# DeltaNet gate stores of the odd units moved from the ScalarE queue to SyncE, between the weight loads and the small matrix stores

## The chip, the core and the metric

One core of one Trainium2 chip runs the kernel. The metric is the device time in microseconds (us) of one execution; the time before is the median of three runs. One further execution was profiled.

## What is computed

The reference is a trunk of two layers. Each layer has two token mixers side by side, retention and a gated DeltaNet, on a sequence of 1024 tokens with 1024 channels, in float32. Cut to the part that the change touches:

```python
proj = rmsnorm(x, norm_g) @ w_in
(rq, rk, rv, rz, dq, dk, dv, dz, db, da, gr, gd) = jnp.split(proj, _split_points(), axis=-1)
# retention -> o_r;  DeltaNet over 8 heads in chunks -> o_d, with for each chunk
#   L = strict lower part of (k_beta k^T) * decay;  solve (L + I) [u w] = rhs
y = jax.nn.sigmoid(gr) * (o_r @ w_up_r) + jax.nn.sigmoid(gd) * (o_d @ w_up_d)
return x + y @ w_o
```

The two merge gates `gd` and `gr` are columns of the one input projection. They come early and are needed late, at the merge.

## The kernel before

**Tiling.** Activations lie transposed, channels on the 128 partitions and tokens along the row, in two halves of 512 tokens. Each float32 operand is split into a high and a low part, so that a dense block of 128 output channels takes, for each half, 8 channel tiles with three matmuls each (lines 846, 848 and 850): 24 matmuls into one of two PSUM banks, `dense_ps[0]` for half 0 and `dense_ps[1]` for half 1. One weight buffer, `w_raw`, takes a 512 KB weight block. ScalarE copies it to `w_hi` (line 1409) and GpSimd makes `w_lo` (line 2543); then `w_raw` is free for the next load.

**Units.** The DeltaNet has 8 heads of two halves, so 16 units in each layer. `unit_schedule` writes out the order of the work for all engines: while the scan of one unit runs (steps `ks`, `xu`, `so` for each of its four chunks), the solve of the next unit is prepared, and pieces of dense blocks fill TensorE in between. Even units (of the schedule) carry the dense blocks K, Z, Q of the next head; odd units carry V, D, R, where D is the DeltaNet merge gate `gd` and R the retention merge gate `gr`.

**The gates.** ScalarE takes a tanh of each half of D and R out of PSUM into the buffer `gate_t[:, half, :]` (line 1521) and then frees the PSUM bank. The buffer is shared by D, R and Z, so each tanh first waits (`gt_st[half]`) until the store of what lay there has landed. The stores go to the scratch tensor `gate_dram` in DRAM, 256 KB each. In the odd units the two D stores are issued by ScalarE itself right behind the tanh (line 1526), the two R stores by SyncE (line 744).

**The small matrices.** Of each chunk the solve needs the 16x16 diagonal blocks of L. VectorE computes them (line 2159, signal `nl_ok`), SyncE writes them to DRAM with eight 4 KB DMAs (`l_store`, line 705), waits until they have landed, and loads them again, broadcast over the partitions, with two 256 KB DMAs (`l_load`, line 713). VectorE then runs 15 steps of forward substitution (lines 2244 and 2247), among which it does its part of the scan: line 2263 makes `uu`, for which the matmul of step `xu` waits (line 1162), and line 2278 updates the state.

**SyncE's queue** works strictly in program order, waits included. For head h it is, in `unit_loads`: weight load Q, row load, weight loads V and D, blocks of unit 2h+2, weight load R, row load, the weight loads m+6 and m+7 (K and Z of the next head; Z or a retention block for the last), blocks of unit 2h+3, and the two R stores. "Odd matrix" below is the set of blocks of unit 2h+3. There are 7 such heads in each layer, so 14 in all. A weight load waits until `w_lo` of the block before it is ready (line 635).

Of the kernel before, what the change touches and what calls it, by code (L numbers as in the profile page):

```python
# [23 lines left out]
HALF = 512  # L24
NHALF = SEQ // HALF
# [3 lines left out]
DH = 8  # L29
# [252 lines left out]
def build(nc, x, norm_gain, w_in, conv_w, a_log, dt_bias, dn_gain, w_up_ret, w_up_dn, w_out, final_gain,  # L282
          masks, rope, ret, out):
    ctx = ExitStack()
    with ctx:
# [3 lines left out]
        def signal(name, per):  # L289
            s = Signal(ctx.enter_context(nc.semaphore(name)), per)  # L290
            signals.append(s)
            return s
# [39 lines left out]
        def ar(name, shape, dt=F32):  # L332
            n = int(np.prod(shape[1:]))
            a = place["at"]
            place["at"] = a + n
            assert place["at"] <= ARENA, (name, place)
            if dt is F32:
                v = arena[:, a:a + n]
                if len(shape) == 3:
                    v = v.rearrange("p (a b) -> p a b", a=shape[1])  # L340
                if len(shape) == 4:
                    v = v.rearrange("p (a b c) -> p a b c", a=shape[1], b=shape[2])
                return v
            return nc.alloc_sbuf_tensor_at(name, shape, dt, offset=arena_at + 4 * a)
# [8 lines left out]
        gate_t = ar("gate_t", [P, 2, HALF])  # L353
# [134 lines left out]
        gate_dram = nc.dram_tensor("gate_scratch", [2, KT, P, SEQ], F32)  # L488
# [43 lines left out]
        gt_ok = signal("gate_tanh_ready", 4)  # L532
        gt_st = [signal("gate_stored0", 32), signal("gate_stored1", 32)]
# [82 lines left out]
        def w_src(t, what, col=0):  # L616

            return what[t, :, bass.ds(col, P)].rearrange("(k p) n -> p k n", p=P)
# [3 lines left out]
        def _(eng):  # L622
# [9 lines left out]
            def load_w(g, src, other=False, ahead=0):  # L632

                eng.wait_ge(w_lo_ok.sem, w_lo_ok.after(g, -ahead))
                eng.dma_start(w_from[other][:, :, :], src).then_inc((w2_in if other else w_in_ok).sem, 16)
# [41 lines left out]
            for l in range(DEPTH):  # L677
# [12 lines left out]
                def row_load(h, b):  # L690

                    u = (l * (2 * DH) + (2 * h + b))
                    eng.wait_ge(m_ok.sem, m_ok.after(u, 0))
                    eng.wait_ge(egc_ok.sem, egc_ok.after(u, 0))
                    eng.dma_start(gcb, row_dram[bass.ds(h, 1), b * HALF:(b + 1) * HALF].to_broadcast([P, HALF]))\
                       .then_inc(row_in.sem, 16)

                def l_store(u, half):

                    t = (l * (2 * DH) + u)  # L700
                    eng.wait_ge(nl_ok.sem, nl_ok.after(t, 1))
                    eng.wait_ge(l_in.sem, l_in.after(t, 0))
                    for a in range(NB if u else NB // 2):
                        seg = slice(BASE * a, BASE * (a + 1))
                        eng.dma_start(l_dram[a].rearrange("c i k -> i c k"), nl[half][seg, :, seg]).then_inc(l_st.sem, 16)

                def l_load(u):

                    t = (l * (2 * DH) + u)
                    eng.wait_ge(l_st.sem, l_st.after(t, 16 * NB))  # L710
                    eng.wait_ge(sv_s.sem, sv_s.after(t, 0))
                    for c in range(0, CPH, 2):
                        eng.dma_start(lb[:, c:c + 2, :], l_source(c)).then_inc(l_in.sem, 16)

                def l_blocks(u, half):
                    l_store(u, half)
                    l_load(u)
# [7 lines left out]
                def unit_loads(h, more):  # L725
                    m = (n + h * 6)
                    load_w(m + BLK_HEADS + 2, w_src(l, w_in, DQ0 + P + h * P))
                    row_load(h + 1, 0)
                    load_w(m + BLK_HEADS + 3, w_src(l, w_in, DV0 + P + h * P))
                    load_w(m + BLK_HEADS + 4, w_src(l, w_in, GD0 + P + h * P))  # L730
                    l_blocks(2 * h + 2, 0)
                    load_w(m + BLK_HEADS + 5, w_src(l, w_in, GR0 + P + h * P))
                    row_load(h + 1, 1)
                    if more:
                        load_w(m + BLK_HEADS + 6, w_src(l, w_in, DK0 + 2 * P + h * P))
                        load_w(m + BLK_HEADS + 7, w_src(l, w_in, DZ0 + P + h * P))
                    else:
                        load_w(m + BLK_HEADS + 6, w_src(l, w_in, DZ0 + P + h * P))
                        load_w(m + BLK_HEADS + 7, w_src(l, w_in, RK0))
                    l_blocks(2 * h + 3, 1)  # L740
                    hc = l * DH + h + 1
                    for b in range(NHALF):
                        eng.wait_ge(gt_ok.sem, gt_ok.after(hc, 3 + b))
                        eng.dma_start(gate_dram[1, bass.ds(h + 1, 1), :, b * HALF:(b + 1) * HALF]
                                      .rearrange("k p t -> p (k t)"), gate_t[:, b, :]).then_inc(gt_st[b].sem, 16)

                for h in range(DH - 2):
                    unit_loads(h, True)
# [588 lines left out]
        def _(eng):  # L1337
# [53 lines left out]
            for l in range(DEPTH):  # L1391
                n = l * NBLK

                def raw_evac(g, t, i):

                    j, b = i // 2, i % 2
                    eng.wait_ge(dense_ok[b].sem, dense_ok[b].after(g, 1))
                    eng.wait_ge(conv_s.sem, conv_s.after(t, 8 if j == 2 else 0))
                    eng.activation(raw[:, j % 2, 3 + b * HALF:3 + (b + 1) * HALF], dense_ps[:, b, :], ACT.Copy)\  # L1399
                       .then_inc(raw_ok.sem, 1)  # L1400
                    eng.wait_ge(raw_ok.sem, raw_ok.after(t, i + 1))
                    eng.sem_inc(dense_free[b].sem, 1)
# [67 lines left out]
                def delta_unit(kind, h):  # L1470

                    b = 0 if kind in ("even", "even_last") else 1
# [5 lines left out]
                    t = (l * (2 * DH) + (2 * h + b)) if kind != "first" else None  # L1478
                    hn = (l * DH + (h + b))
                    hz = (l * DH + h) if kind != "first" else None  # L1480
                    hc = (l * DH + (h + 1))
                    for step in unit_schedule(kind):
# [17 lines left out]
                        elif what == "evac":  # L1500
                            blk, of, half = step[1:]
                            gg = g + (g0 + blk)
                            if of in "KQV":
                                raw_evac(gg, hc, 2 * "KQV".index(of) + half)
                            elif of == "Z":

                                eng.wait_ge(dense_ok[half].sem, dense_ok[half].after(gg, 1))
                                eng.wait_ge(sz_ok.sem, sz_ok.after(hn, 0))
                                eng.wait_ge(gt_st[half].sem, gt_st[half].after(hc, 0))
                                eng.activation(gate_t[:, half, :], dense_ps[:, half, :], ACT.Tanh, scale=0.5)\  # L1510
                                   .then_inc(zt_ok.sem, 1)
                            elif of in "DR":

                                a = "DR".index(of)
                                if kind == "first" and a and half:
                                    eng.wait_ge(w_lo_ok.sem, w_lo_ok.after(n + BLK_HEADS + 1, 0))
                                    eng.dma_start(w_raw[:, :, :], w_src(l, w_in, DZ0)).then_inc(w_in_ok.sem, 16)
                                eng.wait_ge(dense_ok[half].sem, dense_ok[half].after(gg, 1))
                                eng.wait_ge(sz_ok.sem, sz_ok.after(hc, 0))
                                eng.wait_ge(gt_st[half].sem, gt_st[half].after(hc, 16 * a))  # L1520
                                eng.activation(gate_t[:, half, :], dense_ps[:, half, :], ACT.Tanh, scale=0.5)\
                                   .then_inc(gt_ok.sem, 1)
                                eng.wait_ge(gt_ok.sem, gt_ok.after(hc, 2 * a + half + 1))
                                eng.sem_inc(dense_free[half].sem, 1)
                                if kind == "first" or a == 0:
                                    eng.dma_start(gate_dram[a, bass.ds(h + 1, 1), :, half * HALF:(half + 1) * HALF]
                                                  .rearrange("k p t -> p (k t)"), gate_t[:, half, :])\
                                       .then_inc(gt_st[half].sem, 16)
                            elif of in ("rk", "rq"):
                                ret_swap(l * RH, gg, ("rk", "rq").index(of), half)  # L1530
                            else:
                                ret_v(l * RH, gg, int(of[2]), half)
# [179 lines left out]
                for i in range(NHALF * KT):  # L1712
                    b, j = i // KT, i % KT
# [1026 lines left out]
```

## Time and profile before

| | |
|---|---|
| median of 3 runs | 2662.98 us (2661.4 to 2663.35) |
| profiled execution, its own time | 2656.2 us |
| its span, first to last instruction | 2654.4 us |
| TensorE (PE) busy | 2636.3 us, 99% |
| VectorE (DVE) busy | 1728.7 us, 65% |
| GpSimd (POOL) busy | 818.7 us, 31% |
| ScalarE (ACT) busy | 686.0 us, 26% |
| granted TensorE clock | 0.999 |
| DMA queue q1 (SyncE) | 159.07 MB |
| DMA queue q10 (ScalarE) | 56.15 MB |

How to read it: a share is the time in which an engine had work, over the whole span. In a list of waits a row says who waited, for whom, how long in total, how often, and the longest. In a timeline a row has the start, the time from the first to the last of its instructions, the engine, the line and operation with output and inputs, the count, and in brackets idle time of the engine just before, with what ended it. SPq and ACTq are DMA issues in the queues of SyncE and ScalarE, PEld is TensorE's weight load. Matmuls are pipelined: each row of PE overlaps the next, and starts lie some 0.23 us apart in a dense block.

### The profile page before, as it was taken

How to read it: one execution, taken by the hardware profiler on the slowest of the kernel's cores; microseconds unless marked ns; L12 is line 12 of the kernel's file. 1: busy time of each engine (PE TensorE's matmuls, PEld its weight loads, DVE VectorE, ACT ScalarE, POOL GpSimd, SP SyncE). 2: the span in 40 equal slices, each digit the busy share in tenths (PEclk: the TensorE clock that was granted, in tenths of full speed). 3: DMA queues.
4: the chain of work that ended last, by engine and by line, in shares of the span. 5: the costliest groups of instructions: out<-in, count | busy, mean ns of one | idle time of the engine just before them, and what ended most of it. 6: DMA issues, size and time to landing. Idle time of an engine off the chain costs nothing.

```text
span 2654.4 us, 40007 instructions
## 1 busy us (share of the span) xinstructions
PE 2636.3 (99%) x14874; PEld 2256.0 (85%) x14874; DVE 1728.7 (65%) x3866; ACT 686.0 (26%) x1376; POOL 818.7 (31%) x451
## 2 busy tenths in 40 slices
PE   8999999999999999999999999999999999999998
PEld 6888888888898899888878888888888998898887
DVE  7878777877756655434578778777877555563333
ACT  5323233333212222200143333333232221231001
POOL 3123333333312212434512332332323122232453
PEclk9999999999999999999999999999999999999999
DMA  5321223122211112433533222222222111133344
GB/s 174 98 85 55 83 65 89 53 85 65 84 40 53 32 42 71 129 97 117 163 91 95 68 76 66 72 77 69 69 69 78 45 50 43 40 106 99 98 137 151
DMA packets 293413, 217.77 MB, mean 82 GB/s; under 512 B 31746, under 2 KB 246100, under 8 KB 292964
## 3 DMA queue, kind: packets, MB, share of 16 engines
q1 hardware_dynamic: 259620, 159.07, 20.7%
q10 hardware_dynamic: 33600, 56.15, 6.2%
q8 instruction: 119, 1.95, 0.3%
q14 instruction: 74, 0.61, 0.1%
HBM read 176.30 MB, written 38.86 MB: 81 GB/s over the span
## 4 chain that ended last, share of the span: by engine, by line
PE 96%; DVE 1%; DMA 1%; ACT 1%; issue 0%; SPq 0%; POOL 0%; DVEq 0%; ACTq 0%
PE dense_ps L846 24%; PE dense_ps L850 23%; PE dense_ps L848 23%; PE work L829 3%; PE dense_ps L870 2%; PE dense_ps L871 2%; PE dense_ps L872 2%; PE work L1125 1%; PE work L1084 1%; PE work L1162 1%; PE work L1182 1%; PE work L1101 1%; PE work L1151 1%; PE work L1175 1%; PE work L1121 1%; PE work L1136 1%
## 5 line engine op out<-in xcount | busy, mean ns | idle before, releaser
L846 PE MATMUL dense_ps<-act_hi,w_hi 128*128 128x512 f32 x2552 | 1049.3, 411 | 0.8 <-POOL act_lo L2564 0.7
L850 PE MATMUL dense_ps<-act_hi,w_lo 128*128 128x512 f32 x2552 | 999.3, 392 | 0.0
L848 PE MATMUL dense_ps<-act_lo,w_hi 128*128 128x512 f32 x2552 | 997.5, 391 | 0.0
L2543 POOL TENSOR_TENSOR w_lo<-w_raw,w_hi 128x1024 fp32r<-128x1024 f32 x162 | 399.6, 2467 | 1004.8 <-ACT w_hi L1409 562.3
L850 PEld LDWEIGHTS dense_ps<-act_hi,w_lo 128*128 128x128 f32 x2552 | 479.4, 188 | 106.5
L846 PEld LDWEIGHTS dense_ps<-act_hi,w_hi 128*128 128x128 f32 x2552 | 481.3, 189 | 84.6 <-POOL act_lo L2564 2.3
L848 PEld LDWEIGHTS dense_ps<-act_lo,w_hi 128*128 128x128 f32 x2552 | 481.9, 189 | 79.3 <-issue 0.5
L1943 DVE SCALAR_TENSOR_TENSOR arena<-arena,cols 128x512 f32<-128x512 f32 x288 | 240.5, 835 | 5.2
L1409 ACT ACTIVATE w_hi<-w_raw 128x1024 fp32r<-128x1024 f32 x94 | 99.1, 1054 | 329.9 <-PE dense_ps L850 310.8
L1399 ACT ACTIVATE arena<-dense_ps 128x512 f32<-128x512 f32 x96 | 57.2, 596 | 270.1 <-PE dense_ps L850 270.1
L829 PE MATMUL work<-mk,arena 128*128 128x128 f32 x768 | 112.2, 275 | 7.9 <-DMA arena<-in_x 7.9
L1957 DVE SCALAR_TENSOR_TENSOR arena<-arena 128x512 f32<-128x512 f32 x96 | 112.0, 1166 | 11.2 <-ACT arena L1415 10.9
L2244 DVE TENSOR_TENSOR arena<-arena 128x60 f32<-128x60 f32 (+14 forms) x480 | 99.6, 208 | 20.8 <-DMA arena<-l_scratch 8.4
L2630 POOL TENSOR_TENSOR arena<-arena,negh 128x4 f32<-128x4 f32 x32 | 38.7, 1211 | 240.8 <-DVE arena L2150 240.8
L872 PE MATMUL dense_ps<-v_later_lo,act_hi 128*128 128x256 f32 x384 | 107.9, 281 | 0.0
L870 PE MATMUL dense_ps<-v_later_hi,act_hi 128*128 128x256 f32 x384 | 107.9, 281 | 0.0
L871 PE MATMUL dense_ps<-v_later_hi,act_lo 128*128 128x256 f32 x384 | 107.9, 281 | 0.0
L829 PEld LDWEIGHTS work<-mk,arena 128*128 128x128 f32 x768 | 91.9, 142 | 17.7 <-issue 5.1
L2247 DVE TENSOR_TENSOR arena<-arena 128x60 f32<-128x60 f32 (+14 forms) x480 | 92.5, 193 | 16.5
L846 PE MATMUL dense_ps<-o_hi,w_hi 128*128 128x512 f32 x256 | 99.6, 389 | 0.0
L848 PE MATMUL dense_ps<-o_lo,w_hi 128*128 128x512 f32 x256 | 99.6, 389 | 0.0
L850 PE MATMUL dense_ps<-o_hi,w_lo 128*128 128x512 f32 x256 | 99.6, 389 | 0.0
(257 smaller groups left out, 4014.8 us busy)
## 6 DMA issues: line engine op xcount, KB each, us to landing
w_raw<-in_w_in SPq DMA_DIRECT2D x138, 512.0 KB, 3.8
arena<-l_scratch SPq DMA_DIRECT2D x64, 256.0 KB
arena<-gate_scratch ACTq DMA_DIRECT2D x64, 256.0 KB, 2.8
gate_scratch<-arena ACTq DMA_DIRECT2D x36, 256.0 KB, 2.0
w_raw<-in_w_out SPq DMA_DIRECT2D x18, 512.0 KB, 3.7
o_scratch<-arena ACTq DMA_DIRECT2D x32, 256.0 KB, 2.0
w_raw<-in_w_up_dn SPq DMA_DIRECT2D x16, 512.0 KB, 3.7
arena<-o_scratch ACTq DMA_DIRECT2D x32, 256.0 KB, 3.6
```

The source lines that it names most:

```text
L829: mm = eng.transpose(wk[bank][:, c * P:(c + 1) * P], src, ident)
L846: eng.matmul(dense_ps[:, to, :], w_hi[:, slot, k, :], hi[:, k, seg], start=(k == 0), stop=False)
L848: eng.matmul(dense_ps[:, to, :], w_hi[:, slot, k, :], lo[:, k, seg], start=False, stop=False)
L850: mm = eng.matmul(dense_ps[:, to, :], w_lo[:, slot, k, :], hi[:, k, seg], start=False, stop=(k == KT - 1))
L870: eng.matmul(dst, act_hi[:, k, tok], hi[:, k, :], start=(k == 0), stop=False)
L871: eng.matmul(dst, act_lo[:, k, tok], hi[:, k, :], start=False, stop=False)
L872: mm = eng.matmul(dst, act_hi[:, k, tok], lo[:, k, :], start=False, stop=(k == KT - 1))
L1409: eng.activation(w_hi[:, slot, :, :], w_raw[:, :, :], ACT.Copy).then_inc(w_hi_ok.sem, 1)
L1943: eng.scalar_tensor_tensor(out=acc[:, i % 2, :], in0=src, scalar=wcol, in1=acc[:, i % 2, :], op0=ALU.mult, op1=ALU.add).then_inc(conv_s.se ...
L1957: eng.scalar_tensor_tensor(out=kqv[:, i // 2, i % 2 * HALF:(i % 2 + 1) * HALF], in0=th[:, i % 2, :], scalar=1.0, in1=acc[:, i % 2, :], op0 ...
L2244: eng.tensor_tensor(xm[:, :, 0:left], column, xs[:, :, k:k + 1].to_broadcast([P, CPH, left]), ALU.mult).then_inc(sv_s.sem, 1)
L2543: eng.tensor_tensor(w_lo[:, slot, :, :], w_from[second][:, :, :], w_hi[:, slot, :, :].bitcast(F32), ALU.subtract)\
```

## The change

The two D stores of every odd unit are no longer issued by ScalarE. SyncE issues all four gate stores: the two of D behind the weight load m+7 and ahead of the blocks of the odd matrix, the two of R behind these as before. The first unit of a layer keeps its four stores on ScalarE. Sizes, destinations and counts stay.

```diff
@@ SyncE, unit_loads
+                    hc = l * DH + h + 1
+
+                    def gate_store(a, b):
+                        eng.wait_ge(gt_ok.sem, gt_ok.after(hc, 2 * a + b + 1))
+                        eng.dma_start(gate_dram[a, bass.ds(h + 1, 1), :, b * HALF:(b + 1) * HALF]
+                                      .rearrange("k p t -> p (k t)"), gate_t[:, b, :]).then_inc(gt_st[b].sem, 16)
+
+                    gate_store(0, 0)
+                    gate_store(0, 1)
                     l_blocks(2 * h + 3, 1)
-                    hc = l * DH + h + 1
-                    for b in range(NHALF):
-                        eng.wait_ge(gt_ok.sem, gt_ok.after(hc, 3 + b))
-                        eng.dma_start(gate_dram[1, bass.ds(h + 1, 1), :, b * HALF:(b + 1) * HALF]
-                                      .rearrange("k p t -> p (k t)"), gate_t[:, b, :]).then_inc(gt_st[b].sem, 16)
+                    gate_store(1, 0)
+                    gate_store(1, 1)
@@ ScalarE, delta_unit, D and R
-                                if kind == "first" or a == 0:
+                                if kind == "first":
                                     eng.dma_start(gate_dram[a, bass.ds(h + 1, 1), :, half * HALF:(half + 1) * HALF]
```

## Rows read from the trace of the kernel before

**Rows 1.** The page: the span, and TensorE's busy time, share and instructions.

```profile
span 2654.4 us, 40007 instructions
PE 2636.3 (99%) x14874; PEld 2256.0 (85%) x14874; DVE 1728.7 (65%) x3866; ACT 686.0 (26%) x1376; POOL 818.7 (31%) x451
```

**Rows 2.** Timeline of SyncE's queue around the end of one odd unit.

```profile
339.99 19.22 SPq L635 DMA_DIRECT2D w_raw<-in_w_in  x2
359.31 3.80 SPq L705 DMA_DIRECT2D l_scratch<-arena  x8
364.15 1.21 SPq L713 DMA_DIRECT2D arena<-l_scratch  x2
365.41 0.93 SPq L744 DMA_DIRECT2D gate_scratch<-arena  x2
```

**Rows 3.** Timeline of ScalarE, same unit: second D store, tanh of R's halves.

```profile
353.71 0.33 ACTq L1526 DMA_DIRECT2D gate_scratch<-arena  x1
...
359.48 0.60 ACT L1521 ACTIVATE arena<-dense_ps 128x512 f32<-128x512 f32 x1 [2.45 <-PE dense_ps L850]
364.93 0.60 ACT L1521 ACTIVATE arena<-dense_ps 128x512 f32<-128x512 f32 x1 [4.84 <-PE dense_ps L850]
```

**Rows 4.** Timeline of GpSimd and VectorE, same unit: `w_lo`, blocks, first solve step, `uu`.

```profile
356.41 2.39 POOL L2543 TENSOR_TENSOR w_lo<-w_raw,w_hi 128x1024 fp32r<-128x1024 f32 x1
...
356.61 1.11 DVE L2159 SCALAR_TENSOR_TENSOR arena<-work,arena 128x128 f32<-128x128 f32 x4
...
371.12 0.26 DVE L2244 TENSOR_TENSOR arena<-arena 128x60 f32<-128x60 f32 x1 [0.28 <-DMA arena<-l_scratch]
...
376.53 0.34 DVE L2263 SCALAR_TENSOR_TENSOR arena<-work,arena 128x128 f32<-128x128 f32 x1
```

**Rows 5.** Timeline of TensorE, same unit: first matmul of K, and step `xu`.

```profile
364.73 0.39 PE L846 MATMUL dense_ps<-act_hi,w_hi 128*128 128x512 f32 x1
...
377.04 0.39 PE L850 MATMUL dense_ps<-act_hi,w_lo 128*128 128x512 f32 x1
377.27 0.38 PE L1162 MATMUL work<-arena 128*128 128x128 f32 x2
```

**Rows 6.** Issue to landing, minimum, median, maximum: R stores, ScalarE's gate stores, load m+7.

```profile
DMA to landing us min/median/max: 5.1/6.0/6.4
...
DMA to landing us min/median/max: 2.0/2.0/5.4
...
DMA to landing us min/median/max: 3.7/3.7/3.7
```

**Rows 7.** Two stretches of 1 us, same unit; the last columns are clock, DMA share, GB/s.

```profile
361.00:362.00 1.00, 1.00 (x6) 0.81 (x5) 0.00 (x0) 0.00 (x0) 0.00 (x0) 1.00 1.11 305
...
364.00:365.00 1.00, 1.00 (x6) 0.81 (x6) 0.00 (x0) 0.07 (x1) 0.00 (x0) 1.00 0.00 0
```

**Rows 8.** VectorE's waits in the stretches of the 14 odd matrices, one layer each.

```profile
DVE arena L2244 <- DMA arena<-l_scratch: 1.3, 3, 0.6
DVE arena L2244 <- DMA arena<-l_scratch: 1.4, 3, 0.8
```

**Rows 9.** Timeline, odd unit with the longest such wait: solve start, `uu`, step `xu`.

```profile
1593.24 0.26 DVE L2244 TENSOR_TENSOR arena<-arena 128x60 f32<-128x60 f32 x1 [0.81 <-DMA arena<-l_scratch]
...
1598.66 0.34 DVE L2263 SCALAR_TENSOR_TENSOR arena<-work,arena 128x128 f32<-128x128 f32 x1
...
1598.63 0.39 PE L850 MATMUL dense_ps<-act_hi,w_lo 128*128 128x512 f32 x1
1599.06 0.49 PE L1162 MATMUL work<-arena 128*128 128x128 f32 x2
```

**Rows 10.** Timeline, last odd matrix of layer 2: solve start, step `xu`.

```profile
2040.56 0.26 DVE L2244 TENSOR_TENSOR arena<-arena 128x60 f32<-128x60 f32 x1 [0.42 <-DMA arena<-l_scratch]
...
2047.31 0.49 PE L1162 MATMUL work<-arena 128*128 128x128 f32 x2 [0.40 <-DVE arena L2263]
```

**Rows 11.** Timeline of VectorE, an odd matrix without such a wait: solve start.

```profile
281.26 0.24 DVE L2244 TENSOR_TENSOR arena<-arena 128x60 f32<-128x60 f32 x1
```

## The prediction

> **What bounds the kernel now.** I read the page first. TensorE is busy for 2636.3 of 2654.4 us [rows 1], and the granted clock is full. Nothing that only frees another engine can shorten this; a change moves the time if it makes TensorE wait, or removes one of its few waits. So I read next, unit by unit, how close the other engines come to making it wait, on SyncE's queue, then ScalarE, VectorE and TensorE in the same stretch. The odd unit at 340 to 378 us stands for the 14. SyncE issues the weight load m+7 as the second of the two in the first row, at 359.21 - 0.38 = 358.83 us, once `w_lo` is done (356.41 + 2.39 = 358.80) [rows 2, 4]. The eight block stores follow at once, although their data were ready at 357.72 [rows 2, 4]. They take 3.80 us to issue, 1.04 us pass until they have landed, and the block loads are issued at 364.15 to 365.36. The solve starts at 371.12, and VectorE had waited 0.28 us for just these loads [rows 4]. This is the reading that matters: **the chain load m+7, block stores, block loads, solve has no slack of its own on VectorE** in this unit. Over the 14 odd matrices such a wait stands in six, 1.3 + 1.4 = 2.7 us together [rows 8].
>
> How much of it TensorE sees: among the solve steps VectorE makes `uu`, at 376.53 to 376.87, and the matmul of `xu` starts at 377.27, one pitch of 0.23 us behind the matmul ahead of it, so with no wait [rows 4, 5]. In the unit with the longest wait, 0.81 us, `uu` ends at 1599.00 and `xu` starts at 1599.06, where 1598.63 + 0.23 = 1598.86 was due: 0.20 late [rows 9]. So a gap up to 0.61 us is free there, and beyond it each part is paid by TensorE; the matmul then also shows 0.49 instead of 0.38 us [rows 5, 9], which I count as 0.11 more. The last matrix of a layer has other VectorE work in front, and there 0.42 us of gap goes with 0.40 us of TensorE idle [rows 10]: no part is free.
>
> **The change part by part.** Per odd unit it removes two DMA issues from ScalarE (0.33 us each, [rows 3]) and adds two to SyncE.
>
> *ScalarE's part.* 28 x 0.33 = 9.2 us of issue go from an engine that is busy 26% of the time [rows 1] and has idle time of 2.45 and 4.84 us ahead of the next two tanh [rows 3]. Since TensorE waits for none of that, I take nothing. The bound is a gain of 9.2 us if all of it stood on the path; no row shows any of it there.
>
> *SyncE's part.* The D halves have long been converted when SyncE gets past load m+7 (the second store was issued at 353.71 before [rows 3]), so the two added waits cost nothing. The two issues do: two R stores from SyncE take 0.93 us [rows 2], and with the semaphore waits between I take 1.0 us. The bounds are 2 x 0.33 = 0.65 us (ScalarE's price, [rows 3]) and 1.1 us. I stay with SyncE's own row, as the same instruction on the same queue. Queued behind them are the block stores, which were ready 1.1 us before they were issued, so that they move by the full 1.0 us; behind them the wait for their landing, the block loads, and the R stores. The next weight load is issued 3 us after the R stores and isn't moved. The DMA engines show a share of 0.00 from 364 to 365 [rows 7], so the block stores aren't held back by anything that a later issue would dodge: they land 1.0 us later, the loads too.
>
> *The stores' place.* They queue behind the 512 KB of load m+7, which lands 3.7 us after its issue, at 362.5 [rows 6]. 256 KB at the 305 GB/s of the best stretch [rows 7] are 0.86 us, so the D stores land near 363.4 and 364.3. The first is awaited by R's first tanh, at 359.48 now, which must be done before the first matmul of block K at 364.73 [rows 3, 5]: it may start at about 364.0. So the tanh slips by 4 us and hides in the 4.84 us of idle, with 0.6 us to spare. The second tanh is due at 364.93, with 0.6 us to spare also. For the landing the bounds are 2.0 us (a gate store alone) and 6.4 us (an R store behind the block loads) after issue [rows 6]. My value lies between, since only the weight load is ahead. Before, the same stores ran when the engines were empty. On this the Trainium skill, page DMA: Bandwidth & Descriptors, section Issuing engines are not separate DMA queues, says that DMAs of all issuing engines share the same 16 engines, so that another issuer saves only the issue time of its sequencer. The 2.0 against 6.0 us agree if the difference is what lay ahead [rows 6]. By that rule the change hands issue time to the sequencer that has none to spare, which is the same sum.
>
> **The sum.** With every gap 1.0 us longer, a regular unit pays gap + 1.0 - 0.61 + 0.11 = gap + 0.5.
> - Five regular units with a visible gap: 2.7 less 0.42 for the last matrix is 2.3 us; 2.3 + 5 x 0.5 = 4.8, less the 0.3 that the 0.81 us unit pays already: 4.5 us.
> - Seven regular units without a wait in the list. There the loads landed some unknown time before the solve. One began its solve at 281.26 [rows 11], so its landing lies before that. The visible ones are nearest, so I take 0.1 us ahead, 0.4 us each: 2.8 us. Bounds 0 and 0.5 each.
> - The last matrices, where nothing is free: 1.0 and, without a visible gap, 0.9 (bounds 0.5 and 1.0): 1.9 us.
>
> Together 9.2 us. The profiled execution's own 2656.2 us would be 2665.4; it lies 6.8 us under the median of the runs, and I add the sum to the median: 2662.98 + 9.2 = 2672.2 us. TensorE's stalls do not give back anything later, since every later step of TensorE is in order and already dense.
>
> **The rivals.**
> - *A, the forecast*: the block stores leave later and TensorE waits at `xu`. With an issue price of 0.9 to 1.1 us and landings that scatter by 0.3 us, 2668.5 to 2679.
> - *B, not slower by what can be measured*: the delay is smaller than the slack. If the issue costs ScalarE's price, the delay is 0.65 us, and the sum is 2.3 + 5 x 0.15 - 0.3 = 2.8, plus 7 x 0.15 = 1.0, plus 0.65 and 0.5: 5 us, so 2668. If in addition the block loads land faster, because load and R stores meet less of the next weight load, up to all of it is hidden: 2663. For it speaks that eight of the 14 show no wait. Against it, that the row of SyncE says 0.93, and that six are at the edge. It decides below a delay of 0.65 us.
> - *C, the stores' landing*: if the D stores land like the R stores, 6.4 us after 359.31, R's first tanh starts at 365.7 in place of the permitted 364.0: 1.7 us in each of 14 units, 24 us, so 2687. The block path would then hide behind it. Or the block stores' completion waits for the D stores: with the second D store landing at 366.2 the loads are issued 1.05 us later than I say, 14 x 1.05 + 9.2 = 24 us, again 2687. It decides once the D stores land later than 4.7 us after their issue. The same page of the Trainium skill, section Queues, rings and completion order, says that a DMA's semaphore write lands only after every earlier write of that DMA engine. By that rule the big stores ahead could hold the small ones' signals; no row of before has a big write ahead of the block stores.
> - *D, faster*: ScalarE's 9.2 us are worth something. Bound 2654, no row speaks for it.
>
> **How the numbers follow.** A 0.69, B 0.21, C 0.07, D 0.03. The predicted time is that of A. Everything under 5.3 us (0.2%) either way is about what a measurement of this kernel cannot tell from no change. A and C give slower, B gives same: slower 0.75 (with the part of B that lies at its upper end and less the low end of A), same 0.22, faster 0.03. The range goes from 2664, which takes in the larger part of B, to 2682, which takes in A with all its upper bounds and leaves C out.
>
> **What would show it.** Right: in each of the 14 units SyncE's first block store starts some 1.4 to 1.5 us after load m+7's issue instead of 0.48; the list of waits has VectorE line 2244 waiting for the block loads in all 14, 12 to 17 us together instead of 2.7; TensorE or its weight load waits at line 1162 for line 2263 in nearly all of them; the tanh of R's first half starts some 4.5 us after load m+7's issue, with no idle time of TensorE at the first matmul of K. Wrong: a block store less than 0.7 us later (B), the D stores landing over 4.7 us after issue or the wait for the block stores much over 1.04 us (C), or a gap at line 2244 that grew by 1 us while TensorE shows no wait at line 1162, which would mean that I took VectorE's slack too small.

## The result

The changed kernel takes 2676.88 us (median of 4, 2675.96 to 2678.66) beside 2662.19 us before (median of 4): the ratio is 1.0065, with a 95% interval of 1.0053 to 1.0077, so 14 to 20 us slower. The two profiled executions, 2656.2 and 2675.96 us, lie 19.8 us apart. The forecast was slower by 9.2 us, to 2672.2 us in a range of 2664 to 2682: the direction and the range hold, and the size was taken more than a third too small (9.2 us beside 14.7 us by the medians and 17.3 us by the ratio).

The page after, answering to [rows 1]:

```profile
span 2674.2 us, 40007 instructions
PE 2642.4 (99%) x14874; PEld 2252.2 (84%) x14874; DVE 1729.5 (65%) x3866; ACT 686.2 (26%) x1376; POOL 818.3 (31%) x451
```

The share of busy time hides the loss: 99% both times. TensorE's busy time grew by 6.1 us with the same instructions. Of this, 6.0 us stand at steps `ks` and `xu`: a matmul that comes late is itself longer (0.38 for 0.27 us at `xu`), and it no longer overlaps the one ahead of it. TensorE's list of waits has the rest of the loss. Before, this list had only one wait of 0.4 us for line 2263 among the solve steps. Lines from 744 on are shifted by 6, so 1157 is the old 1151 (step `ks`), 1168 the old 1162 (step `xu`), 2250 the first operation of the solve (2244), 2269 makes `uu` (2263) and 2284 updates the state (2278). TensorE's waits after, over the span, without those of the start:

```profile
PE work L1157 <- DVE arena L2284: 7.0, 13, 1.1
PE work L1168 <- DVE arena L2269: 5.7, 14, 0.4
```

Both wait for VectorE operations that stand among the solve steps, which start late. VectorE's waits for the block loads in the stretches of the 14 odd matrices, answering to [rows 8]:

```profile
DVE arena L2250 <- DMA arena<-l_scratch: 14.1, 7, 2.6
...
DVE arena L2250 <- DMA arena<-l_scratch: 12.5, 7, 2.3
```

26.6 us in all 14 units, in place of 2.7 us in six. Where they come from stands in SyncE's queue, same unit as [rows 2], and the next line is VectorE's first solve step, as in [rows 4]:

```profile
342.88 19.21 SPq L635 DMA_DIRECT2D w_raw<-in_w_in  x2
362.14 1.05 SPq L744 DMA_DIRECT2D gate_scratch<-arena  x2
363.29 4.12 SPq L705 DMA_DIRECT2D l_scratch<-arena  x8
368.60 1.21 SPq L713 DMA_DIRECT2D arena<-l_scratch  x2
369.86 0.94 SPq L744 DMA_DIRECT2D gate_scratch<-arena  x2
...
375.39 0.26 DVE L2250 TENSOR_TENSOR arena<-arena 128x60 f32<-128x60 f32 x1 [1.66 <-DMA arena<-l_scratch]
```

Load m+7 is issued at 342.88 + 19.21 - 0.38 = 361.71. Counted from there, and beside [rows 2]: the block stores start at 1.58 us (0.48 before), they take 4.12 us (3.80 before), and from their end to the block loads 1.19 us pass (1.04 before). So the block loads leave 6.89 us after load m+7, 5.32 before: 1.57 us later, and only 1.10 of that is the two D stores and the waits between them. The rest is new: **the same eight stores are slower to issue and slower to land behind the D stores' data.** Two stretches of 1 us show why (columns as in [rows 7]):

```profile
365.00:366.00 1.00, 1.00 (x6) 0.83 (x5) 0.00 (x0) 0.00 (x0) 0.00 (x0) 1.00 1.12 404
366.00:367.00 1.00, 1.00 (x6) 0.82 (x5) 0.00 (x0) 0.37 (x1) 0.00 (x0) 1.00 0.83 235
```

These are 3.3 to 5.3 us after load m+7. The same time in the kernel before, 362 to 364 us, was nearly free of data:

```profile
362.00:364.00 2.00, 2.00 (x10) 1.68 (x9) 0.00 (x0) 0.00 (x0) 0.00 (x0) 1.00 0.13 12
```

Now the DMA engines are full just when the block stores go out. In each of the 14 units one of the eight issues takes clearly longer; here it is the second, 0.79 us in place of 0.43.

The landings show it too. The first line is the first block store of this unit before, the next two are the second D store and the first block store after:

```profile
DMA to landing us min/median/max: 3.3/3.3/3.3
...
DMA to landing us min/median/max: 4.4/4.4/4.4
...
DMA to landing us min/median/max: 3.9/3.9/3.9
```

Before, the first block store lands at 359.31 + 3.3 = 362.6, together with load m+7 (358.83 + 3.7 = 362.5). After, it lands at 363.29 + 3.9 = 367.2, together with the second D store (362.76 + 4.4 = 367.2). In all 14 units it lands within 0.25 us of the load before, and within 0.2 us of the second D store after. The others follow, at first some 0.2 us apart. Before, they have caught up at the last store, which lands 1.46 us after its issue (median); in the change it takes 1.80 us.

R's first tanh, as in [rows 3]:

```profile
366.63 0.60 ACT L1527 ACTIVATE arena<-dense_ps 128x512 f32<-128x512 f32 x1 [6.72 <-DMA gate_scratch<-arena]
367.81 0.60 ACT L1527 ACTIVATE arena<-dense_ps 128x512 f32<-128x512 f32 x1 [0.58 <-PE dense_ps L856]
```

It waits for the D store until 366.63, 4.92 us after load m+7 and 4.5 us after the issue of the store. TensorE's list has no wait on ScalarE for the bank that it frees. The landing fits, as forecast, but with little to spare: in 13 of the 14 units the tanh starts 4.9 to 5.3 us after load m+7, and TensorE does not stand still. In the last odd unit of the first layer it starts at 5.38 us, and there TensorE is idle for 0.12 us at the next dense block, too short for the list, with the matmul some 0.3 us late. The trace shows nothing else that this tanh costs TensorE.

### The profile page after: what moved, and what is told of

Its sections match the earlier page's. It is cut to its first block, busy times and chain, and to the rows that moved or that the text cites. A ratio compares the mean times of both kernels' runs of the same rounds, so it can differ in the third digit from the quotient of the medians.

```text
span 2674.2 us, 40007 instructions
## 1 busy us (share of the span) xinstructions
PE 2642.4 (99%) x14874; PEld 2252.2 (84%) x14874; DVE 1729.5 (65%) x3866; ACT 686.2 (26%) x1376; POOL 818.3 (31%) x451
## 4 chain that ended last, share of the span: by engine, by line
PE 81%; DVE 6%; DMA 5%; SPq 3%; POOL 2%; issue 1%; ACT 1%; DVEq 0%; ACTq 0%; POOLq 0%
PE dense_ps L852 20%; PE dense_ps L856 19%; PE dense_ps L854 19%; DMA arena<-l_scratch 4%; PE dense_ps L876 2%; PE dense_ps L877 2%; PE dense_ps L878 2%; PE work L835 2%; SPq L705 2%; PE work L1131 1%; DVE arena L2250 1%; POOL w_lo L2549 1%; DVE arena L2253 1%; PE work L1090 1%; DMA l_scratch<-arena 1%
## 5 line engine op out<-in xcount | busy, mean ns | idle before, releaser
L1963 DVE SCALAR_TENSOR_TENSOR arena<-arena 128x512 f32<-128x512 f32 x96 | 112.1, 1168 | 11.3 <-ACT arena L1421 10.9
L835 PEld LDWEIGHTS work<-mk,arena 128*128 128x128 f32 x768 | 91.9, 142 | 17.6 <-issue 5.1
```

The costliest lines, as they stand in the source:

```text
L835: mm = eng.transpose(wk[bank][:, c * P:(c + 1) * P], src, ident)
L1963: eng.scalar_tensor_tensor(out=kqv[:, i // 2, i % 2 * HALF:(i % 2 + 1) * HALF], in0=th[:, i % 2, :], scalar=1.0, in1=acc[:, i % 2, :], op0 ...
```

## The experiments

Each is a kernel of its own, timed beside the kernel before on the same chip. "Gaps" below is the sum of VectorE's idle time right before the first solve step of the 14 units, and "block loads" the mean time from the issue of load m+7 to that of the first block load; both are read from the traces of all 14 units, one execution each. The gaps include those too short for the lists of waits. Three theories were set against each other: *issue* (SyncE's time ahead of the block stores counts), *data* (the D stores' 512 KB ahead of or beside the block stores count) and *tanh* (R's tanh, held by the landing, counts).

| kernel | ratio to before (95%) | medians, us over before | block stores start | block loads leave | gaps |
|---|---|---|---|---|---|
| before | | | 0.50 | 5.43 | 2.9 |
| the change | 1.0065 (1.0053 to 1.0077) | 14.7 | 1.58 | 7.05 | 26.5 |
| the change again | 1.0066 (1.0052 to 1.0080) | 18.0 | 1.58 | 7.01 | 24.2 |
| two small DMAs | 1.0031 (1.0020 to 1.0041) | 8.7 | 1.58 | 6.38 | 16.1 |
| two of 256 KB | 1.0089 (1.0074 to 1.0105) | 24.2 | 1.58 | 7.29 | 30.0 |
| four small DMAs | 1.0104 (1.0078 to 1.0129) | 27.0 | 2.52 | 7.56 | 35.9 |
| one of 448 KB | 1.0067 (1.0050 to 1.0085) | 18.8 | 1.10 | 6.90 | 22.4 |
| two of 256 KB by ScalarE | 1.0012 (1.0003 to 1.0022) | 4.1 | 0.50 | 6.19 | 10.7 |
| second half only | 1.0026 (1.0017 to 1.0036) | 7.3 | 1.10 | 6.48 | 15.3 |
| D stores early | 1.0001 (0.9993 to 1.0010) | 0.1 | 0.48 | 5.38 | 0.8 |
| D stores between | 1.0080 (1.0066 to 1.0093) | 21.2 | 0.48 | 5.38 | 0.0 |
| block stores first | 0.9999 (0.9990 to 1.0008) | -0.2 | | | 0.0 |
| D early, blocks first | 0.9991 (0.9982 to 1.0000) | -0.3 | | | 0.0 |

**Two small DMAs.** The issue alone: two 4 KB DMAs of constants at the place of the D stores, which stay on ScalarE.

```diff
+                    for b in range(2):
+                        eng.wait_ge(gt_ok.sem, gt_ok.after(l * DH + h + 1, min(b, 1) + 1))
+                        eng.dma_start(probe_dram[(l * (DH - 1) + h) * 2 + b], mk[:, 0:8]).then_inc(probe, 16)
                     l_blocks(2 * h + 3, 1)
```

> The kernel before, with two more DMAs of 4 KB (constants to a scratch tensor of their own) issued by SyncE at the place where the change puts the D stores; the D stores stay on ScalarE. Theory 'issue' (the time that SyncE takes to issue ahead of the block stores is what counts): block stores start 1.0 to 1.1 us later after load m+7, block loads 1.0 to 1.2 us later, VectorE's gap at the solve grows by as much in all 14 units, time 9 to 11 us over before. Theory 'data' (the 512 KB ahead of the block stores in the queue count): block loads move by less than half of what the change moved them (1.6 us), time 0 to 4 us over before. Theory 'tanh' (R's first tanh, held by the landing of the D store, counts): the tanh is not held, time as before within 2 us.

```profile
360.74 0.38 SPq L637 DMA_DIRECT2D w_raw<-in_w_in  x1
361.17 1.05 SPq L744 DMA_DIRECT2D probe_scratch<-mk  x2
362.32 3.66 SPq L707 DMA_DIRECT2D l_scratch<-arena  x8
367.03 1.21 SPq L715 DMA_DIRECT2D arena<-l_scratch  x2
```

The queue of the same unit has the same 1.05 us of issue as in the change, but the block stores take 3.66 and not 4.12 us. The ratio makes 8.2 us, the medians 8.7, just under the 9 to 11 us expected: about half of the change's loss. Issue alone accounts for half, and the tanh theory, by which this run should equal before, cannot have this half. (The parts do not simply add, since whichever comes first uses up the slack.)

**Two of 256 KB.** The same with `mk[:, 0:512]` and a wider scratch tensor: issue and data, but no tanh that waits for them.

> As the run with two small DMAs, but each is 256 KB, as large as a D store; the D stores stay on ScalarE and R's tanh does not wait for the added ones. Theory 'issue': the same time as with the two small ones, 9 to 11 us over before. Theory 'data': the full loss of the change, 14 to 15 us over before (profile: block loads 1.6 us later, line 713 waiting longer than 1.04 us). Theory 'tanh': as before within 2 us, since no tanh is held. Both of the first two together: 10 us for the small, 15 for the full ones.

Against the small ones nothing but the data differs. The block loads leave 0.91 us later still, the gaps grow by 13.9 us and the time by some 15 us. Data count beside issue. No tanh waited, so the tanh is not needed to explain the change's loss. But the loss is larger than the change's and than the 15 us expected. Part of this is three late units, told under the next run. In the other eleven the block loads leave at 6.99 us (7.05 in the change) with gaps of 1.90 us each (1.89 in the change), so there the added 512 KB do just what the D stores do. The three late units have some 3.4 us of gap beyond that, of a difference of 6.3 us by the ratios; the rest stays open.

**Four small DMAs.** The count raised from two to four, nothing else.

> The kernel before, with four more DMAs of 4 KB (constants to a scratch tensor) issued by SyncE ahead of the block stores in place of two. Once the slack is used up, every us must cost a us: issue 2.1 to 2.2 us, block loads 2.0 to 2.1 us later than before, a regular unit pays gap + 2.05 - 0.5. From the two small ones (1.0 us later, about 9 us over before) one more us in each of 14 units gives 14 us on top: 22 to 25 us over before. If the loss were not on this chain, twice the issues would cost twice the loss of two, 16 to 19 us, or less.

The block stores start 0.94 us later than with two, and the time rises by 18 us, above the 14 expected; in all it is 27 us over before, where 22 to 25 were expected. It is also above twice the loss of two. Each us on the chain costs at least a us once its slack is gone.

The excess over 14 us is in part three late units. In the 4th, 10th and 14th unit the block loads leave at 8.4 to 8.8 us, in the other eleven at 7.2 to 7.5. In the 4th unit, the page's DMA part for the two us in which the last block stores should land (461 to 463 us) has a line that the undisturbed 5th (552 to 554) has not:

```profile
q8 instruction: 1, 0.02, 3.0%
```

It is one packet of 16 KB on a queue that the profile calls "instruction". Ten units in five of these kernels have such a packet between the block stores and the time when the last one would have landed: the three here, the same three with two of 256 KB, the 4th and 10th with the second half only, and the 10th with two small DMAs and with two of 256 KB by ScalarE. In all ten the block loads leave 0.5 to 1.5 us later than the mean of the other units of the same run. In 13 more units, those of the change among them, it comes at most 0.5 us before the block loads or behind them, and they are not late. So a shift of the block stores can also move them into a transfer that no line of the kernel issues. This is read from single traces; no run varies it. It doesn't explain all: the gaps of the eleven undisturbed units grew by 1.3 us each for block loads 0.97 us later.

**One of 448 KB.** One issue with nearly the data of both stores:

```diff
+                    eng.dma_start(probe_dram[l * (DH - 1) + h], mk[:, 0:896]).then_inc(probe, 16)
                     l_blocks(2 * h + 3, 1)
```

> The kernel before, with one more DMA of 448 KB issued by SyncE ahead of the block stores: nearly the data of two D stores, with one issue. The D stores stay on ScalarE. Theory 'issue': block stores 0.5 to 0.6 us later and block loads as much, time 2 to 4 us over before. Theory 'data' added to 'issue': block stores 0.5 to 0.6 us later, but block loads 1.0 to 1.3 us later, through slower issue of the block stores and a longer wait for their landing; time 8 to 13 us over before.

```profile
360.91 0.38 SPq L637 DMA_DIRECT2D w_raw<-in_w_in  x1
361.33 0.58 SPq L742 DMA_DIRECT2D probe_scratch<-mk  x1
362.01 4.13 SPq L707 DMA_DIRECT2D l_scratch<-arena  x8
367.70 1.21 SPq L715 DMA_DIRECT2D arena<-l_scratch  x2
```

The block stores start only 0.60 us later than before, yet take 4.13 us, and 1.56 us pass to the loads where the small ones had 1.05. The block loads leave 1.47 us later, 0.87 of it data. That is more than I had given the data (0.4 to 0.8 us), and the loss, 17.8 us by the ratio where 8 to 13 were expected, is as large as the change's own. Merging the two stores into one issue would have saved nothing, as far as these runs go.

**Two of 256 KB by ScalarE.** The data without any issue on SyncE, behind R's first tanh:

```diff
+                                if kind == "odd" and a and half == 0:
+                                    for i in range(2):
+                                        eng.dma_start(probe_dram[(l * (DH - 1) + h) * 2 + i], mk[:, 0:HALF])\
+                                           .then_inc(probe, 16)
```

> The kernel before, with two more DMAs of 256 KB issued by ScalarE right behind R's first tanh, some 1.3 us after load m+7, on ScalarE's queue: the data of the D stores beside load m+7 and the block stores, with no issue on SyncE. Theory 'issue': block stores and loads as before, time as before within 2 us. Theory 'data', if it is the DMA engines' load that counts, whoever issues: block loads 0.4 to 0.8 us later at an unchanged start of the block stores, 2 to 7 us over before. If it counts only within SyncE's own queue, as before within 2 us.

```profile
361.46 0.38 SPq L637 DMA_DIRECT2D w_raw<-in_w_in  x1
361.94 4.30 SPq L707 DMA_DIRECT2D l_scratch<-arena  x8
367.59 1.21 SPq L715 DMA_DIRECT2D arena<-l_scratch  x2
```

The block stores start at their old time and take 4.30 instead of 3.80 us. The loads leave 0.76 us later, for 4.1 us. The data count whoever issues them, so it is not their place in SyncE's queue, but that they move at the same time. That only 4 us come of 14 x 0.76 is the slack at work: six of the 14 gaps stay under 0.61 us. The landings follow the order of issue over both queues, nearly: the third block store, the first issued behind an added one, lands within 0.2 us of it in all 14 units.

**Second half only.** The first D store stays on ScalarE.

```diff
-                    gate_store(0, 0)
                     gate_store(0, 1)
                     l_blocks(2 * h + 3, 1)
...
-                                if kind == "first":
+                                if kind == "first" or (a == 0 and half == 0):
```

> The change with half of it done: only the store of D's second half is moved to SyncE, the first half stays with ScalarE. Theory 'issue': block stores 0.5 to 0.6 us later, block loads 0.6 to 0.8 us later; a regular unit pays gap + delay - 0.5, so 3 to 7 us over before, less than half of the change's 14.7 since the slack is used up once. Theory 'data': the same size, but with the delay mostly behind the block stores, at line 713's wait. Theory 'tanh': R's first tanh is not held at all, the second waits at most 0.2 us: time as before within 2 us.

0.60 us of issue and 0.45 us behind it. As the ratio has it, 6.9 us, at the upper edge of what was expected. R's first tanh isn't held here at all, which again leaves the tanh without a share.

**The change again.**

> The changed kernel once more, unaltered, beside the other arrangements of this set, to have its loss and its stretch on the same chip. 13 to 18 us over before; block loads 1.6 us later after load m+7 than before (7.0 instead of 5.4 us), VectorE's gaps at the solve 24 to 29 us in the 14 units.

The loss on this chip is 17.5 us by the ratio and 18.0 by the medians, at the upper end of what was expected, with the same delays.

**D stores early.** The change with the D stores ahead of load m+7.

```diff
+                    gate_store(0, 0)
+                    gate_store(0, 1)
                     load_w(m + BLK_HEADS + 7, w_src(l, w_in, DZ0 + P + h * P))
-                    gate_store(0, 0)
-                    gate_store(0, 1)
                     l_blocks(2 * h + 3, 1)
```

> The change with one place altered: SyncE issues the two D stores ahead of the weight load m+7, where its queue waits for some 19 us anyway, and not behind it. Theory 'issue' and theory 'data': the block stores start 0.48 us after load m+7 as before, and the time is that of before within 3 us; the same holds for 'tanh', as the stores land at once. If ScalarE's 28 issues (0.33 us each) are worth something, up to 9 us under before. If it is stores issued by SyncE as such, wherever they stand, that cost: 10 to 15 us over before.

The time is that of before (the interval goes from -1.9 to +2.7 us). That SyncE issues the stores costs nothing that can be measured, and that ScalarE no longer does brings nothing; the place is the whole loss.

**D stores between** block stores and block loads, where SyncE waits anyway.

```diff
-                    gate_store(0, 0)
-                    gate_store(0, 1)
-                    l_blocks(2 * h + 3, 1)
+                    l_store(2 * h + 3, 1)
+                    gate_store(0, 0)
+                    gate_store(0, 1)
+                    l_load(2 * h + 3)
```

> The change with the two D stores put between the block stores and the block loads, where SyncE waits 1.0 us for the landing anyway. Their issue is then hidden (block loads 5.4 to 5.8 us after load m+7), but the D stores leave at 4.3 us in place of 0.5 us and can land no earlier than 6.4 us after load m+7, while R's first tanh may start at 5.2 at the latest. Theory 'issue' alone (landing doesn't count): time within 4 us of before. Theory 'tanh' (late landing blocks ScalarE, which blocks TensorE's bank): TensorE waits 1.5 to 2.5 us at the first matmul of K in each of 14 units, 20 to 35 us over before. I expect the second: the landing is harmless in the change only because it just fits.

TensorE's waits over the span, then the tanh and the first matmul of K in one unit:

```profile
PE dense_ps L853 <- ACTq L1531: 18.9, 14, 1.7
```

```profile
368.82 0.60 ACT L1528 ACTIVATE arena<-dense_ps 128x512 f32<-128x512 f32 x1 [8.40 <-DMA gate_scratch<-arena]
...
369.61 0.47 PE L853 MATMUL dense_ps<-act_hi,w_hi 128*128 128x512 f32 x1 [1.33 <-ACTq L1531]
```

The chain of the blocks is as before and the gaps are zero, but the tanh starts 6.6 to 6.9 us after load m+7 and TensorE stands at block K in all 14 units, 18.9 us. This is the mechanism of rival C, brought about by the later place: it costs 21 us, and the change misses it only by the few tenths read above.

**Block stores first**, on the kernel before, and **D early, blocks first**, the same on the run with the D stores early.

```diff
-                    load_w(m + BLK_HEADS + 7, w_src(l, w_in, DZ0 + P + h * P))
-                    l_blocks(2 * h + 3, 1)
+                    l_store(2 * h + 3, 1)
+                    load_w(m + BLK_HEADS + 7, w_src(l, w_in, DZ0 + P + h * P))
+                    l_load(2 * h + 3)
```

> The kernel before with the block stores of the odd matrices issued ahead of load m+7, which then goes into the wait for their landing. If the chain of the blocks is what TensorE feels, shortening it can only win back what before still loses: the block stores start 1.1 us earlier, block loads about 1.1 to 1.5 us earlier, VectorE's gaps at the solve go to zero in all 14 units, and 0 to 3 us are gained. If load m+7, now 2.8 us later, becomes the late one (its block's copy on ScalarE waits for it), the gain is lost or turns into a loss of up to 5 us.

> The change with both places altered: D stores issued by SyncE ahead of load m+7, where it is idle, and the block stores also ahead of load m+7. No gap at the solve in any odd unit; as the run with the block stores first, 0 to 3 us under before, if ScalarE's issues are worth nothing. If they are worth something it is 2 us or more better than that run.

SyncE's queue of the first, same unit:

```profile
357.28 3.76 SPq L705 DMA_DIRECT2D l_scratch<-arena  x8
361.08 0.43 SPq L635 DMA_DIRECT2D w_raw<-in_w_in  x1
362.07 1.21 SPq L713 DMA_DIRECT2D arena<-l_scratch  x2
```

The block loads leave 2 us earlier, and in this run the gaps vanish in all 14 units. It gains nothing that can be measured. The second has no gaps either, and it has a ratio of 0.9991 whose interval ends at 1.0000, while its median is 0.3 us under before. I call neither a gain: before, the slack was hardly used up, so there was nearly nothing to win back.

## Why the prediction was right in direction and short in size

- *What bounds the kernel, and which chain is next*: right. All of the loss appears at `ks` and `xu`, for VectorE operations among late solve steps.
- *The conversion of a gap into TensorE time* (free up to 0.61 us, then the excess and 0.11 us; everything in the last matrix): right, and better than it had a right to be, as its 0.61 us came from one unit. Put the gaps of the 14 units of each trace into it, less what before pays already, and it gives, beside the loss by the ratio in brackets, 19.8 us for the change (17.3; the two profiled executions differ by 19.8), 17.5 for the change again (17.5), 9.4 for two small DMAs (8.2), 23.3 for two of 256 KB (23.7), 29.2 for four small (27.7), 15.7 for one of 448 KB (17.8), 9.2 for the second half only (6.9) and 4.5 for the data by ScalarE (3.2). So it is within 2.5 us of the ratios; beside the spans of the profiled executions themselves it is within 3.9 us.
- *SyncE's issue, 1.0 us*: it was 1.08 us to the start of the block stores. ScalarE's 0.33 us, the lower bound, turned out to be the price of a store with nothing right ahead of it in the queue, whichever engine: with the D stores early, SyncE issues them in 0.33 us each too. Behind load m+7 the first takes 0.58 us. With issue alone, the run with two small DMAs gave gaps of 16.1 us and a loss of 8.2 us; the sum of the forecast was 9.2 us. So the forecast is the loss of that kernel, not of this one.
- *The step that failed* is the sentence that the block stores aren't held back by anything, because the DMA share is 0.00 from 364 to 365 [rows 7]. It read the engines as they were, and left out that the moved stores bring 512 KB into just this time: I costed the D stores' own landing behind load m+7, at 363.4 and 364.3, and did not set that beside the block stores, which run from 360.3 to 364.1 by the same sum. The term had to be 1.6 us, of which 0.5 to 0.6 are data: slower issue of the eight stores (4.12 for 3.80 us) and a longer wait for their landing (1.19 for 1.04 us in the unit shown, 0.3 us in the mean). With 1.6 us in place of 1.0 the same sum gives 9.2 + 14 x 0.6 = 17.6 us, beside 17.3 and 17.5 us by the ratios of the change's two sets of runs.
- *The units without a visible gap*: taken at 0.4 us each, with a bound of 0.5. Their bound held the landings right, but not the delay, and all seven show gaps of 1.3 us and more in the change.
- *Rows misread*: that no row of before has a big write ahead of the block stores isn't so. Load m+7 writes 512 KB and stands right ahead of them, and before the change the first block store already lands with it. The data were ready 1.6 us before the block stores were issued and not 1.1 us (this is the distance to load m+7), which leaves the sum as it is. And rival B's seven units leave out their 0.1 us of lead, 0.7 us too much.
- *The landing of the D stores*: forecast for the first at 363.4 with load m+7 at 358.83, so 4.6 us after it; measured 4.8 to 5.2 us, with a wait of TensorE in one unit of 14, 0.12 us. Rival C stays out, but by less than the 0.6 us I gave it. Its second half, that the small stores' signals wait for the big ones, happened in a small way. On this the Trainium skill, page DMA: Bandwidth & Descriptors, section Queues, rings and completion order, says that a semaphore write lands only after every earlier write of that DMA engine, across its queues. The traces agree in that the first block store lands together with the second D store, and in that ScalarE's stores delay SyncE's block stores too. But in some units the first block store's landing is shown up to 0.17 us ahead of the D store's, so whether it is this rule or plain sharing of the engines, no run here tells.
- *ScalarE's part, nothing*: right (the run with the D stores early).
- *Rival B*: fell, as the delay was 1.6 and not 0.65 us.

Open: why one or two of the eight block stores take longer to issue while other data move, and how the 0.5 to 0.9 us of data divide between slower issue and later landing from case to case. The second half only has an unchanged issue time (3.75 us in the unit shown below) and a wait of 1.38 us behind it, the 448 KB have both longer.

```profile
359.33 0.58 SPq L744 DMA_DIRECT2D gate_scratch<-arena  x1
360.01 3.75 SPq L705 DMA_DIRECT2D l_scratch<-arena  x8
365.14 1.21 SPq L713 DMA_DIRECT2D arena<-l_scratch  x2
```

## What to carry to other kernels

A DMA that nobody waits for soon still costs twice where it is put ahead of a latency chain: its issue time on that queue, and its data in the time of the small transfers that follow. When a transfer is moved, lay its data beside everything that will then run at the same time, not beside the engines as they were. Put such stores where the queue waits for long anyway. Check the other end as well: a buffer that is reused soon makes a late store stop the engine that reuses it. And read such a chain unit by unit: a mean of 14 can hide three that met a transfer of another kind.

## What the runs showed of the hardware

- What a store costs to issue went by what stood right ahead of it in its queue, and not by the engine or the size. A gate store of 256 KB took 0.33 us with nothing right ahead, on ScalarE (before) and on SyncE (D stores early); on SyncE it took 0.58 us right behind load m+7 and 0.42 to 0.46 us behind another store. ScalarE's second added store, right behind its first, took 0.46 us. Two of 4 KB and two of 256 KB at the same place both took 1.05 us.
- Eight small stores of 4 KB took 3.66 us to issue after two small DMAs and 3.80 us before, but 4.05 to 4.30 us while 448 to 512 KB of other stores were moving, on either queue. With 256 KB it was 3.75 us (all in the third unit).
- A small store landed no sooner than the big transfer issued just ahead of it in the same queue, to within 0.25 us: with the 512 KB of load m+7 before, with the second D store in the change, in all 14 units of each.
- A 16 KB packet of the queue that the profile calls "instruction" among the block stores went with block loads 0.5 to 1.5 us later, in ten units of ten.
- A matmul of `xu` that TensorE had to wait for showed about 0.1 us more than one without a wait: 0.49 in place of 0.38 us for a pair, 0.38 in place of 0.27 us for one. The conversion with this 0.11 us fits the eight runs named above to 2.5 us or better.
